# A gated MLP's up-projection by seven block products instead of eight, with its results kept in DRAM

## The reference, cut to what matters

```python
x = x + g1 * mix                                   # mix = concat(attn_out, u) @ w_out
h2 = modulate(rms_norm(x, norm_ffn_w[l]), sh2, sc2)
up = depthwise_conv(h2 @ w_up[l], ffn_conv_w[l], ffn_conv_b[l])   # width 3 over positions
gate, val = jnp.split(up, 2, axis=-1)
x = x + g2 * ((jax.nn.silu(gate) * val) @ w_down[l])
```

## Time and profile before

| what | value |
|---|---|
| runs | 1313.53, 1313.84, 1316.81 us; median 1313.84 |
| the profiled execution | 1318.48 us, its span 1316.7 us |
| mean granted TensorE clock | 0.972 |
| PE busy | 1236.6 us, 94% of the span, 6181 matmuls |
| DVE busy | 692.7 us, 53% |
| ACT, POOL busy | 448.3 us, 34%; 127.8 us, 10% |
| moved by DMA | 122.06 MB, 93 GB/s |

### The profile page before, as it was taken

How to read it: one execution, slowest core, us unless ns; L and a number is a source line. 1 busy time by engine, 2 the same in 40 slices (tenths; PEclk the granted TensorE clock), 3 DMA queues, 4 the chain that set the end, 5 groups by cost and what they waited for, 6 DMA issues and landing times. The chain is left out here.

```text
span 1316.7 us, 16038 instructions
## 1 busy us (share of the span) xinstructions
PE 1236.6 (94%) x6181; PEld 1024.3 (78%) x6181; DVE 692.7 (53%) x988; ACT 448.3 (34%) x718; POOL 127.8 (10%) x139
## 2 busy tenths in 40 slices
PE   5899999798998889989999999999999979999997
PEld 1378888798878767878888888888888858887886
DVE  1489987599855444335343434343434344457445
ACT  4542366765556445433222222222222111111110
POOL 2100111055540200000000000000000000004001
PEclk9899999899999689999999999999999989999999
DMA  9222655379992042122111111111111041113112
GB/s 382 73 69 83 137 107 102 97 177 254 257 268 70 0 160 96 65 74 71 48 48 48 48 48 48 48 48 48 48 48 48 0 167 48 48 48 104 48 50 79
DMA packets 85477, 122.06 MB, mean 93 GB/s; under 512 B 6698, under 2 KB 60066, under 8 KB 84404
## 3 DMA queue, kind: packets, MB, share of 16 engines
q1 hardware_dynamic: 75796, 87.65, 20.0%
q0 software_dynamic: 8480, 29.56, 11.4%
q10 hardware_dynamic: 1152, 4.19, 0.8%
HBM read 85.74 MB, written 8.39 MB: 71 GB/s over the span
## 5 line engine op out<-in xcount | busy, mean ns | idle before, releaser
L1433 PE MATMUL ps<-hx,uph 128*128 128x512 f32 x672 | 261.4, 389 | 0.0
L1434 PE MATMUL ps<-hx,uph 128*128 128x512 f32 x672 | 261.4, 389 | 0.0
L1437 PE MATMUL ps<-hx,upl 128*128 128x512 f32 x672 | 206.9, 389 | 0.0
L1235 DVE TENSOR_TENSOR upl<-up_raw,uph 128x1024 fp32r<-128x1024 f32 x44 | 53.8, 1226 | 263.9 <-ACT uph L1232 263.9
L1232 ACT ACTIVATE uph<-up_raw 128x1024 fp32r<-128x1024 f32 x44 | 46.5, 1060 | 339.4 <-PE ps L1437 328.5
L1566 PE MATMUL ps<-dnh,ah 128*128 128x512 f32 x352 | 138.0, 392 | 11.8 <-DVE al L1617 11.8
L1433 PEld LDWEIGHTS ps<-hx,uph 128*128 128x128 f32 x672 | 126.2, 188 | 26.2
L1437 PEld LDWEIGHTS ps<-hx,upl 128*128 128x128 f32 x672 | 126.1, 188 | 26.2
L1434 PEld LDWEIGHTS ps<-hx,uph 128*128 128x128 f32 x672 | 126.1, 188 | 26.2
L1567 PE MATMUL ps<-dnl,ah 128*128 128x512 f32 x352 | 137.7, 391 | 0.0
L1568 PE MATMUL ps<-dnh,al 128*128 128x512 f32 x352 | 137.5, 391 | 0.0
(11 more groups left out here) (239 smaller groups left out, 2141.4 us busy)
## 6 DMA issues: line engine op xcount, KB each, us to landing
up_raw<-in_w_up SPq DMA_DIRECT2D x44, 512.0 KB, 3.8
wm<-in_w_mod SPq DMA_DIRECT2D x32, 512.0 KB, 6.4
sums<-wm POOLq DMA_DIRECT2D x32, 512.0 KB, 8.3
dn_raw<-in_w_down SPq DMA_DIRECT2D x44, 256.0 KB, 2.7
wm<-in_w_mod SPq DMA_DIRECT2D x8, 1024.0 KB, 20.3
conv_y<-u POOLq DMA_DIRECT2D x10, 512.0 KB, 4.5
xs<-in_x ACTq DMA_DIRECT2D x8, 512.0 KB, 13.8
gw_raw<-in_w_in SPq DMA_DIRECT2D x8, 512.0 KB, 4.2
```

Of the source, the lines that this page charges most:

```text
L1235: dve.tensor_tensor(out=upl[:, g], in0=up_raw[:, g], in1=f(uph[:, g]), op=ALU.subtract).then_inc(up_lo, 1)
L1433: pe.matmul(o, uph[:, g, k, :], hx[:, k, 0, c_], start=(k == 0), stop=False)
L1434: pe.matmul(o, uph[:, g, k, :], hx[:, k, 1, c_], start=False, stop=False)
L1437: last = pe.matmul(o, upl[:, g, k, :], hx[:, k, 0, c_], start=False, stop=(k == KT - 1))
```

## The change

The product of the 256 weight columns of a step with 1024 positions is seen as 2 x 2 blocks: the weights A as gate or value (row) by first or second 512 of the model width (column), h as first or second 512 of the model width by first or second 512 positions. Strassen's scheme, in Winograd's form, needs 7 products of half-width blocks instead of 8, and sums of blocks ahead of and behind them.

- Products 1 and 2 have A11 and A12 with parts of hx, product 3 a weight sum with a part of hx; 5, 6, 7 and 4 take sums of h (`t_op`). The sums of h are made once, in the out-projection, by `t_sums` on DVE (four operations per tile from tile 4 on), and split by `t_high` on ACT and `t_low` on DVE. From tile 4 on only half of the tile's h is itself split (`kept`).
- A step's weights need 4 sums (`w_sums`, DVE) and 7 splits of 128 x 512 (`split_high` on ACT, `split_low` on DVE), each with its own buffers.
- PE runs the products in the order 1, 6, 5, 7, 2, 3, 4. Products 2, 3 and 4 accumulate on the banks of 1, 5 and 7, after ACT has copied product 1 (`p1_out`) and DVE has added u4 from the bank of 5 and c22 from the bank of 7.
- Behind them DVE adds u2, u4, c22, c12 and c21 (`add`), the last three into `cg` and `cv` in SBUF, and ACT copies c11. All taps then read SBUF.
- The t_op buffers take hid's place, so hid has only two slots; each step's hid is stored to DRAM (512 KB) and 20 of the 22 tiles come back at the end of the up-projection, in five loads of 2 or 4 tiles.
- The three blocks are one. The first two down steps are split inside up step 21, the first down step takes row tiles 4 to 7 first, x1 is loaded by POOL's queue after down step 7, and the last two steps of a down half are run together, row tile by row tile (6 matmuls per bank).
- x has three buffers in the out-projection instead of four.

```diff
-        NXT = 4
+        NXT = 3
...
+        w_raw = [at(123, "w_raw0", [P, 2, KT, P]), at(51, "w_raw1", [P, 2, KT, P])]
+        s3_sum = at(15, "s3_sum", [P, KH, P])
+        op_kib = {1: (139, 141), 2: (46, 48), 3: (5.5, 7.5), 5: (38, 40), 6: (34, 36), 7: (42, 44)}
+        w_op = {p: [at(kib, f"w_op{p}{v}", [P, KH, P], F32R) for v, kib in enumerate(kibs)] for p, kibs in op_kib.items()}
+        w_op[4] = [piece(v, f"w_op4{v}", [P, KH, P], F32R) for v in range(2)]
+        t_op = {p: [at(59 + 16 * n + 8 * v, f"t_op{p}{v}", [P, KH, HALF], F32R) for v in range(2)] for n, p in enumerate((5, 6, 7, 4))}
...
+        hid = at(51, "hid", [P, FT, T])
+        hid_dram = nc.dram_tensor("hid_scratch", (FT, P, T), F32, kind="Internal").ap()
+        RING = FT - 2
...
+        PRODUCTS = (1, 6, 5, 7, 2, 3, 4)
+        START = [(1, 0), (2, 0), (1, 1), (2, 1), (3, 0), (5, 0), (6, 0), (7, 0), (4, 0), (6, 1), (5, 1), (7, 1), (3, 1), (4, 1)]
+        SPLITS = [(1, 0), (2, 0), (1, 1), (5, 0), (3, 0), (6, 0), (2, 1), (7, 0), (4, 0), (6, 1), (5, 1), (7, 1), (3, 1), (4, 1)]
+        DVE_SPLITS = [(5, 0), (6, 0), (7, 0)]
+        HI_SPLITS = [q for q in SPLITS if q not in DVE_SPLITS]
+        BANK = {1: 0, 2: 0, 6: 1, 5: 2, 3: 2, 7: 3, 4: 3}
...
+            def rows_of(p, k, v):
+                if p == 1:
+                    return hx[:, k, v, 0:HALF]
+                if p == 2:
+                    return hx[:, KH + k, v, 0:HALF]
+                if p == 3:
+                    return hx[:, KH + k, v, HALF:T]
+                return t_op[p][v][:, k, :]
...
+                sp.wait_ge(hid_out[0], 8 * RING)
+                reload(0, 2, hid_in[0])
+                sp.wait_ge(prod, product_at(6, FT - 1))
+                reload(6, 4, hid_in[1])
+                sp.wait_ge(prod, product_at(5, FT - 1))
+                reload(2, 4, hid_in[1])
+                sp.wait_ge(hid_out[1], 8 * RING)
+                reload(18, 2, hid_in[1])
+                sp.wait_ge(prod, product_at(7, FT - 1))
+                reload(10, 4, hid_in[1])
+                sp.wait_ge(dn_split, 2)
+                load_step(2, 1, 0, 0)
+                sp.wait_ge(prod, product_at(4, FT - 1))
+                reload(14, 4, hid_in[1])
...
+                def product(p, j, s, start):
+                    pe.wait_ge(up_lo, split_at(p, j))
+                    for k in range(KH):
+                        for w, v in ((0, 0), (0, 1), (1, 0)):
+                            last = pe.matmul(bank_of(p, s), w_op[p][w][:, k, :], rows_of(p, k, v), start=(start and k == 0 and w == 0 and v == 0),
+                                             stop=(k == KH - 1 and w == 1), skip_group_check=True)
+                    last.then_inc(prod, 1)
...
+                for p, j in START:
+                    if (p, j) == (1, 0):
+                        pe.wait_ge(gated, TT - 1)
+                        pe.wait_ge(h2_lo, TT // 2)
+                    if (p, j) == (1, 1):
+                        turn(TT - 1)
+                        pe.wait_ge(mod5, TT - 1)
+                    if p == 2:
+                        pe.wait_ge(p1_out, j + 1)
+                    if (p, j) == (3, 0):
+                        pe.wait_ge(gated, TT)
+                        pe.wait_ge(h2_lo, TT)
+                    if (p, j) == (5, 0):
+                        pe.wait_ge(p3_out, 1)
+                    if j == 0 and p >= 4:
+                        pe.wait_ge(t_lo, {5: 2, 6: 4, 7: 6, 4: 8}[p])
+                    if (p, j) == (5, 1):
+                        pe.wait_ge(mod5, TT)
+                    if (p, j) == (3, 1):
+                        pe.wait_ge(comb, add_at("u4", 1))
+                    if p == 4:
+                        pe.wait_ge(comb, add_at("c22", j))
+                    product(p, j, j, p != 2 and p != 4 and (p, j) != (3, 1))
+
...
+                def body(j, s):
+                    for p in PRODUCTS:
+                        if p == 1:
+                            pe.wait_ge(c11_out, j - 1)
+                        elif p == 2:
+                            pe.wait_ge(p1_out, j + 1)
+                        else:
+                            pe.wait_ge(comb, {6: add_at("u2", j - 2), 5: add_at("c12", j - 2), 7: add_at("c21", j - 2),
+                                              3: add_at("u4", j), 4: add_at("c22", j)}[p])
+                        product(p, j, s, p not in (2, 3, 4))
+
...
+                        if kind == "last":
+                            before = down_product(half, 1 - s, "next", t)
+                            if t == TT - 1:
+                                before.then_inc(dn_mm, 1)
+                        last = down_product(half, s, kind, t)
+                        if kind == "last":
+                            last.then_inc(bank_mm, 1)
+                        elif t == rows_first[-1]:
+                            last.then_inc(dn_mm, 1)
+
...
+                    if t == TT - 1:
+                        dve.wait_ge(prod, product_at(1, 0))
+                        dve.tensor_copy(p1_first[:], bank_of(1, 0)).then_inc(p1_out, 1)
...
+                        o, a, b, op = ((t1, source(t, slice(0, KH)), h_first[:, 0:KH, e], ALU.subtract),
+                                       (t2, source(t, slice(KH, KT)), t1, ALU.subtract),
+                                       (h_first[:, 0:KH, e], t2, h_first[:, 0:KH, e], ALU.subtract),
+                                       (h_first[:, KH:KT, e], h_first[:, KH:KT, e], t2, ALU.subtract))[n]
+                        dve.tensor_tensor(out=o, in0=a, in1=b, op=op).then_inc(t_sum_done, 1)
...
+                        o, a, b, op = {7: (s3_sum[:], a11, a21, ALU.subtract), 5: (a21, a21, a22, ALU.add),
+                                       6: (a11, a21, a11, ALU.subtract), 3: (a12, a12, a11, ALU.subtract)}[p]
+                        dve.tensor_tensor(out=o, in0=a, in1=b, op=op).then_inc(w_sum, 1)
...
+                def body(j, s, first=False, last=False):
+                    nxt = (j + 1, 1 - s)
+                    dve.tensor_scalar(ffcur[s].unsqueeze(1), ffs[:, bass.ds(j, 1), :], 1.0, None, ALU.mult).then_inc(comb, 1)
+                    add("u2", j, s)
+                    add("u4", j, s)
+                    if first:
+                        t_low(4, 0)
+                        t_low(4, 1)
+                        split_low(4, 0, 0)
+                    if not last:
+                        w_sums(*nxt, (7, 5))
+                        if not first:
+                            split_low(1, *nxt)
+                        w_sums(*nxt, (6,))
+                    add("c22", j, s)
+                    if last:
+                        dve.wait_ge(hid_done, FT - 1)
+                        down_low(0, RING, 0, 0, "first")
+                    else:
+                        for p in (6, 5, 7):
+                            split_low(p, *nxt)
+                        if not first:
+                            split_low(2, *nxt)
+                        w_sums(*nxt, (3,))
+                    add("c12", j, s)
+                    if not last:
+                        split_low(3, *nxt)
+                    side(j, s, 0, False)
+                    add("c21", j, s)
+                    side(j, s, 0, True)
+                    if last:
+                        dve.wait_ge(hid_in[0], 16)
+                        down_low(1, 0, 0, 1, "peeled")
+                    else:
+                        split_low(4, *nxt)
+                    side(j, s, 1, False)
+                    side(j, s, 1, True)
+                    dve.wait_ge(mid_tap, 3 * j + 3)
+                    dve.wait_ge(side_taps, 4 * j + 4)
+                    if first:
+                        dve.wait_ge(t_sum_done, 4 * (TT // 2))
+                        dve.wait_ge(h2_lo, TT)
+                    elif not (isinstance(j, int) and j < 2):
+                        dve.wait_ge(hid_out[s], 8 * (j - s))
+                    dve.tensor_tensor(out=hid[:, RING + s, :], in0=y[:, 0, :], in1=y[:, 1, :], op=ALU.mult).then_inc(hid_done, 1)
...
+                    if t >= TT // 2:
+                        t_sums(t, range(4))
+                        split_low(1, 0, 0)
+                        split_low(2, 0, 0)
+                        w_sums(0, 0, (7, 5, 6, 3))
...
+                pool.wait_ge(dn_mm, 8)
+                pool.dma_start(x1[:], x1_dram.rearrange("(t p) d -> p t d", p=P)).then_inc(x1_in, 16)
```

More of the change, by code:

```diff
@@ L1222, in up_half @@
-        def up_half(pe, g, bank, hh):
-            o, c_ = ps[:, bank, :], slice(hh * HALF, (hh + 1) * HALF)
-            for k in range(KT):
-                pe.matmul(o, uph[:, g, k, :], hx[:, k, 0, c_], start=(k == 0), stop=False)
-                pe.matmul(o, uph[:, g, k, :], hx[:, k, 1, c_], start=False, stop=False)
-                last = pe.matmul(o, upl[:, g, k, :], hx[:, k, 0, c_], start=False, stop=(k == KT - 1))
-            return last
-        def up_split_high(act, g):
```

(43 more changed lines are left out.)

594 lines of the change are left out of this document (353 added, 241 removed).

## The result

Median 1260.64 us (1253.36 to 1265.57, 4 runs) against 1315.32 us for the kernel before on the same chip: ratio 0.9577, 95% interval 0.9519 to 0.9635, so 54.7 us faster (48 to 63). The prediction was 1261.3, from a gain of 52.5. The profiled execution took 1265.57 us, with a span of 1263.8 and a mean granted clock of 0.968.

The account below looks back on a forecast made before the run. PE was taken to stay the bound at 0.2266 us per matmul. The terms -59.8 + 5.1 + 15.6 - 8.9 - 3.9 = -51.9, taken as -52.5 from 1313.84, gave 1261.3 us, range 1253 to 1277.

Parts of the forecast that it names:

- The product removed: Up-projection: 12 matmuls fewer in each of 22 steps, at 0.2266 us each, -59.8 us if PE stays the bound.
- DVE follows: Up-projection loop: DVE's work per step takes 17.8 us (17.3 to 19.3), under PE's 19.04.
- The rival that DVE becomes the bound: Up-projection loop: DVE sets the period, at 19.3 to 20.5 us per step the time is 1266 to 1290; chance 0.17.
- The way in: Out-projection into the loop: DVE's added work stops PE, +1.5 (tile 4), +3.6 (tile 5), +15.6 us from tile 6's transposes.
- the stops named as signs: Way in: PE stops about 5 us before products 2 and 4 of step 0, 3 before product 3 of step 1.
- One block: Joint of up- and down-projection: no gap or slow start there, less 2.0 us for hid's reload: -8.9 us.
- The reload: Early down-projection: weights queued behind hid coming back from DRAM stop PE, 1 us, then 0 to 3; 2.0 us taken.
- The half switch: Between the down-projection's halves: PE loses 2 to 3 us again beside POOL's additions, change 0, possibly 1 us shorter.
- The end: After PE's last matmul: with the last two steps merged only the last bank's work and store remain, -3.9 us.
- The trip through DRAM: Up-projection: the 20 stores of hid lie beside PE work, each with over 9 us to land; no cost.
- A reload that costs more: Rival, shared with a costlier way in: down steps 2 to 5 wait 4 to 10 us, 1266 to 1273; chance 0.13.
- the way in cost less: Rival: DVE's queue overlaps better before the loop and the reload is hidden, up to 8 us less, 1252 to 1257; chance 0.13.

Follow-up runs that it names:

- p1_twice: Changed kernel with product 1 run twice in steps 2 to 21, the same result written again: 1316.24 us.
- dve3: Changed kernel with three more half-width subtractions on DVE in each of steps 1 to 19: 1282.69 us.
- barrier: Changed kernel with the first down step waiting until all of hid is made: 1269.66 us.
- apart: Changed kernel with the last two down steps of each half run one after the other: 1271.53 us.
- stores2: Changed kernel with each hid tile stored twice, into two scratch tensors, all waits waiting for both: 1259.02 us.
- hide: Changed kernel with DVE's block sums of a tile behind the next tile's residual, and first weight splits and sums at tile 3 instead of 5: 1249.46 us.
- dve1: Changed kernel with one more half-width subtraction on DVE in each of steps 1 to 19: 1259.45 us.
- c22: As a run: changed kernel with block c22 of step 0 added right behind the last low parts: 1260.98 us.

## Why the prediction was right

Its mechanism held, and the three large terms were right within 0.6 us each. Three small ones were mis-sized, all to the same side, by about 4 us together. That the median came within 1 us of the number is partly luck: the gain was 2.2 us larger than predicted, and the kernel before took 1.5 more than the 1313.84 from which it was taken off.

- **The product removed** (-59.8). Shown by p1_twice: the 240 matmuls of 20 steps are worth 54.4 in the loop, as by the rate of the earlier trace rows, and 55.0 in all.
- **DVE follows** (17.8, range 17.3 to 19.3). 18.0 by dve3, 1.0 us under PE's 19.04, which is why one operation more was free and three weren't. The rival that DVE becomes the bound was 1 us per step away. The order in the step came out as walked: u4 waits for product 5, c22 is done 3.9 after u4's start (4.0), the last multiply 17.6 after it (18.0). The Trainium skill's rule (VectorE: DVE Perf Modes, "The DRAIN you can't avoid") gave 18.6. The trace agrees only in part: independent operations start 0.61 apart though one lasts 0.69, and those that wait for the one before 0.71 to 0.73 (722.42 to 723.13), so a semaphore that this section of the Trainium skill calls free cost 0.1 here.
- **The way in** (+1.5, +3.6, +15.6). Tile 5's transposes came 13.26 after tile 4's instead of 11.78 (+1.48), tile 6's 17.29 after instead of 13.71 (+3.58). From S to the loop it was 61.0, 61.3 predicted, with (4,0) at S+41.2 (41.1 predicted) and (3,1) at S+54.8 (55.1). One step was told wrongly: up to product (1,1) one slow start of 2.0 was taken, at (2,0), and there were two. The clock was down already at S, after the 5.28 us ahead of tile 6, an idle time that the prediction had at 5.6 but charged no slow clock; that cost 2.45 up to (1,0). It fell again at (2,0), for 1.7. In the sum this hardly shows: PE being late itself, the stop ahead of (2,0) was 3.15 for 5.1, and the copy that ends it came 0.8 later than walked. The slow start at (4,0) cost 2.45 and was absorbed, as predicted, by the wait ahead of (3,1), of which nothing was left. So of the stops named as signs, about 5, 5 and 3, there came 3.15, 4.41 and none.
- **One block** (-8.9). Measured -12.2 with the half switch. The gap and the slow start went (8.1 and 1.8; barrier brings back 9.0 and 2.4). The reload was mis-sized: 2.0 us were taken, and stops of 0.24 and 0.42 came, which cost 1.3 with the longer starts at each. The mechanism was the predicted one at the second: DVE's split waited for ACT, and ACT for the weight, which came at 1033.01 from behind the reload, 14.9 us after the end of step 21. The one before it came at 1026.67, 8.6 after that end where 9 to 10 were predicted, and there DVE, still at the tail of step 21, was the last to be ready. From 1006 to 1031 the DMA moved 408 GB/s, where the estimate by x1 (4.19 MB in 13.0 us) had 322.
- **The half switch** (0). Mis-sized: its stops fell from 2.82 to 0.66, 2.4 us with the longer starts at each. DVE's splits there are as slow beside POOL as before (2.09 and 2.79), but begin 0.8 after PE has started the second half, where they began 2.0 after it, behind eight multiplies in a row (4.87). POOL, which started earlier too, is done at 1148.61, before the last split of the second set (1149.10, 1.21 instead of 2.79), so the second stop of 0.88 is gone. In apart the splits begin at 0.8 as well, but the first of them takes 1.75 beside POOL instead of 0.68; the merged steps save 1.2 of stop there and 1.6 of slow clock.
- **The end** (-3.9). -4.6, of which apart gives back 4.1. The last addition took 0.69, not 1.3, as POOL was idle by then.
- **The trip through DRAM** (0). Shown by stores2 for the stores. No run was made to vary the reload, but dve3 and barrier do: begun 3.0 us later it makes a stop of 3.80, and with 9 us more to run there is none. So it has no time to spare as it stands.

In sum the changed part gained 56.2 by the profiles and 54.7 by the medians, 52.5 predicted. The 3.7 between the first and the last is the reload 0.7, the half switch 2.4 and the end 0.7, less the 0.6 that the sum already held for the half switch, and 0.5 spread over the rest. Of the rivals, the one with DVE as the bound was 1 us per step away. A reload that costs more didn't come, and the way in cost less only once its operations were moved, in hide.

Open: why the clock fell behind the stop of 1.88 in apart and not behind that of 1.94 before the change (the slow matmuls stand there in place of the second stop, 0.88), and why the slow clock on the way in cost 1 us more in the traces of dve1, dve3, p1_twice and stores2, whose instructions up to there are those of the changed kernel (5.49 us for the 12 matmuls of (2,0), 4.54 in the changed kernel).

## What to carry to other kernels

Where an engine is full at full clock, as here, matmuls left out are worth their start-to-start time. One risk lies in whether the next engine can make its round in the new, shorter step, so count its operations by their distance, and test the spare by adding some. The other lies at the edges of such a loop, where there is no spare: 59.8 us of matmuls were left out, some 20 of them were lost on the way in, and hide got 10 of these back. There the place of an operation in the queue counts more than its duration: sums that nobody waits for yet belong behind the operation that the full engine waits for. A stop taken away inside a stretch whose end another chain sets only moves to where that chain is waited for.

## What the runs showed of the hardware

- Three half-width subtractions that wait on each other took 2.14 us together, and each independent one 0.61: self-waits cost 0.1 each, about a sixth of such an operation.
- Whether a stop brings the lower clock isn't told by its length alone: 8 matmuls stood 0.43 apart (1.2 GHz) behind a stop of 1.88 us in apart, none behind 1.94 and 2.20 (ahead of the transposes of tile 7) in the kernel before, and (2,0) was at the lower clock behind one of 1.96 in hide. A stop near 2 us may cost 1.6 us more or nothing, and a rearrangement that shortens one stop and brings another can lose by it, as c22 did.
- The stretch that no kernel here changes, up to the out-projection's first matmul, took 462.95 to 475.0 us in eleven profiled executions. That is wider than most single effects looked for, and cutting the span there made effects of 2 us legible in one trace. Not those of 1 us: behind the cut, four of the runs took 0.9 us more up to (3,1) than the changed kernel, with the same instructions.
- A down weight of 256 KB landed 2.8 us after its issue in the median, and 14.5 after it from behind the reload of hid in the same queue, with the DMA moving 408 GB/s. How far PE is ahead of that queue decides its stops ahead of the third and fourth down step: none in barrier, 0.24 and 0.42 in the changed kernel, 3.80 in dve3.
